# Shift and scale columns of a transformer's modulation made with the weights in the array, from four weight buffers

## What is computed

```python
for l in range(DEPTH):                       # DEPTH = 2
    m_lat = jnp.split(cond_lat @ w_mod[l] + b_mod[l], 6, axis=-1)
    m_ctx = jnp.split(cond_ctx @ w_mod[l] + b_mod[l], 6, axis=-1)
    y_lat, y_ctx = _token_mixing(            # w_in, attention, delta net, HGRN, w_out
        _modulate(x_lat, m_lat[0], m_lat[1]), _modulate(x_ctx, m_ctx[0], m_ctx[1]), ...)
    x_lat = x_lat + m_lat[2] * y_lat
    x_lat = x_lat + m_lat[5] * _expert_choice_ffn(_modulate(x_lat, m_lat[3], m_lat[4]), ...)
    ...                                      # the same for x_ctx, in the first layer

def _modulate(x, shift, scale):
    return _rms(x) * (1 + scale) + shift
```

## Time and profile before

| | us |
|---|---|
| median of 3 runs | 3901.55 |
| lowest, highest | 3899.71, 3906.54 |
| the profiled execution, its own time | 3915.78 |
| its span, first to last instruction | 3914.0 |
| PE busy in the span | 3239.1 |
| PE weight loads busy | 2335.5 |
| DVE busy | 2296.5 |
| ACT busy | 1742.8 |

### The profile page before, as it was taken

How to read it: one execution, slowest core, us unless ns; L and a number is a source line. 1 busy time by engine, 2 the same in 40 slices (tenths; PEclk the granted TensorE clock), 3 DMA queues, 4 the chain that set the end, 5 groups by cost and what they waited for, 6 DMA issues and landing times.

```text
span 3914.0 us, 59293 instructions
## 1 busy us (share of the span) xinstructions
PE 3239.1 (83%) x24115; PEld 2335.5 (60%) x24115; DVE 2296.5 (59%) x2989; ACT 1742.8 (45%) x2289; POOL 359.9 (9%) x100
## 2 busy tenths in 40 slices
PE   6899977766859998989988999787658588888887
PEld 1465767655436666666642566677554466666666
DVE  0140564677247777777741043555782678788887
ACT  1111531223136777767740114422231477777776
POOL 0000000000011112111100000000000122222122
PEclk9999977856979999999999999888558788888888
DMA  7310000001167988889865110000002589898996
GB/s 248 111 49 32 1 1 3 3 2 45 41 238 286 354 333 322 327 322 353 323 244 204 44 54 1 1 3 3 2 33 113 224 327 343 330 347 341 346 347 252
DMA packets 180704, 680.24 MB, mean 174 GB/s; under 512 B 15435, under 2 KB 25759, under 8 KB 180383
## 3 DMA queue, kind: packets, MB, share of 16 engines
q1 hardware_dynamic: 166088, 637.81, 42.9%
q0 software_dynamic: 6144, 20.98, 2.3%
q10 hardware_dynamic: 8283, 18.67, 1.2%
HBM read 656.44 MB, written 20.97 MB: 173 GB/s over the span
## 4 chain that ended last, share of the span: by engine, by line
PE 65%; DVE 14%; DMA 8%; ACT 6%; issue 6%; ACTq 1%; SPq 0%; POOL 0%; DVEq 0%; PEldq 0%
PE ps L1835 14%; PE ps L718 13%; PE ps L1865 11%; PE ps L1290 5%; DMA gu<-in_moe_w_gate 4%; PE ps L1635 4%; PE ps L657 3%; PE ps L1873 2%; PE ps L973 2%; ACT hi L1947 2%; DMA arena<-in_w_mod 2%; DMA gu<-in_moe_w_up 2%; DVE gu_lo L2096 2%; PE ps L951 1%; PE ps L964 1%
## 5 line engine op out<-in xcount | busy, mean ns | idle before, releaser
L2096 DVE TENSOR_TENSOR gu_lo<-gu,hi 128x2816 fp32r<-128x2816 f32 x256 | 781.4, 3086 | 327.7 <-ACT hi L1947 289.5
L1947 ACT ACTIVATE hi<-gu 128x2816 fp32r<-128x2816 f32 x256 | 643.0, 2551 | 192.4 <-DMA gu<-in_moe_w_up 147.7
L1835 PE MATMUL ps<-hi,xsplit 128*96 128x512 f32 (+3 forms) x2304 | 602.3, 410 | 73.7 <-ACT hi L1947 53.0
L1835 PEld LDWEIGHTS ps<-hi,xsplit 128*96 128x96 f32 (+1 forms) x2304 | 425.3, 190 | 198.6 <-ACT hi L1947 63.7
L718 PE MATMUL ps<-arena 128*128 128x512 f32 (+2 forms) x1536 | 503.4, 488 | 7.3 <-PE ps L718 4.5
L2096 DVE TENSOR_TENSOR down_lo<-down,hi 128x1024 fp32r<-128x1024 f32 (+1 forms) x256 | 404.0, 1619 | 64.0 <-ACT hi L1947 64.0
L1835 PE MATMUL ps<-gu_lo,xsplit 128*96 128x512 f32 (+3 forms) x1536 | 400.9, 399 | 40.8 <-DVE gu_lo L2096 40.8
L1947 ACT ACTIVATE hi<-down 128x1024 fp32r<-128x1024 f32 (+1 forms) x256 | 347.5, 1375 | 177.8 <-PE ps L1865 127.5
L718 PEld LDWEIGHTS ps<-arena 128*128 128x128 f32 x1536 | 289.7, 190 | 212.5 <-issue 187.2
L1835 PEld LDWEIGHTS ps<-gu_lo,xsplit 128*96 128x96 f32 (+1 forms) x1536 | 280.2, 188 | 134.4 <-DVE gu_lo L2096 70.9
L2176 POOL DMA_INDIRECT arena<-xn_rows,row_of x32 | 53.2, 1662 | 2158.0 <-DVE row_of L2087 2153.4
(11 more groups left out here) (290 smaller groups left out, 4453.3 us busy)
## 6 DMA issues: line engine op xcount, KB each, us to landing
gu<-in_moe_w_gate SPq DMA_DIRECT2D x256, 704.0 KB, 13.6
gu<-in_moe_w_up SPq DMA_DIRECT2D x256, 704.0 KB, 5.2
down<-in_moe_w_down SPq DMA_DIRECT2D x64, 2048.0 KB, 13.2
arena<-in_w_mod SPq DMA_DIRECT2D x24, 2048.0 KB, 8.1
down<-in_moe_w_down SPq DMA_DIRECT2D x32, 1536.0 KB, 17.3
arena<-in_w_in SPq DMA_DIRECT2D x6, 2048.0 KB, 8.0
arena<-in_w_out SPq DMA_DIRECT2D x4, 2048.0 KB, 10.2
arena<-in_w_in SPq DMA_DIRECT2D x4, 1536.0 KB, 6.8
```

Of the source, the lines that this page charges most:

```text
L1835: ins = nc.tensor.matmul(ps[0:lhs.shape[1], 3 * m + b, 0:n], lhsT=lhs, rhs=w[:, c0 + 512 * b:c0 + 512 * b + n], start=(row == 0 and stage ...
L1947: nc.scalar.activation(hi_part(p, is_last), whole(p), ACT.Copy).then_inc(hi_a.sem, 1)
L2096: nc.vector.tensor_tensor(lo_part(p), whole(p), hi_part(p, is_last).bitcast(F32), ALU.subtract) \
```

## The change

The 12 chunks now have four buffers of their own, `mst`, with a semaphore each, and SP waits for `modmm`, the count of finished chunks, without TensorE's own wait between. The loads of `w_in` wait for the chunks that lie in the same memory (9 and 10). The four gate chunks are multiplied as before. The eight shift and scale chunks are multiplied the other way round: each 128 x 128 block of the weights is the stationary operand and the two conditions are the moving one, so that a chunk is 4 blocks times 8 slices, 32 matmuls with 2 columns each, and the result is already columns over 128 partitions. Their bias is added from `rowsT`, into which `b_mod` is now transposed at the start together with the other small rows, in one DVE step per part; the 32 transposes and `modT` go. DVE does two gate rows, the columns, and the last two gate rows, in this order. On ACT the loads are cut in two: constants, conditions and the `b_mod` rows first, then Silu and the copy, and only then x, ctx and the small parameters. Three constants that nothing reads are dropped.

```diff
-        for g, (src, n) in enumerate(loads(layer)):
...
+                if layer:
+                    sp.wait_ge(used.sem, used.n(layer - 1, USES * NE))
+                for g in range(N_MOD):
+                    if g >= MRING:
+                        sp.wait_ge(modmm.sem, modmm.n(layer, g - MRING + 1))
                     if g == 2:
                         for r in range(2):
                             sp.dma_start(modrow[r:r + 1, :], t["b_mod"][layer:layer + 1, :]).then_inc(bmod.sem, 16)
+                    sp.dma_start(mst[g % MRING], t["w_mod"][layer][:, g * 512:(g + 1) * 512]
+                                 .rearrange("(f p) n -> p f n", p=P)).then_inc(mload[g % MRING].sem, 16)
...
-            for n, (dst, src) in enumerate(ins):
-                act.dma_start(dst, src).then_inc((s_first if n < N_FIRST else s_in).sem, 16)
+            for dst, src in ins[:N_FIRST]:
+                act.dma_start(dst, src).then_inc(s_first.sem, 16)
             act.wait_ge(s_rowsT.sem, 1)
-            nc.scalar.activation(rowsT[:, :], ps[:, 7, 0:84], ACT.Copy).then_inc(s_cond.sem, 1)
             nc.scalar.activation(condT[:, :], ps[:, 7, 68:84], ACT.Silu).then_inc(s_cond.sem, 1)
+            nc.scalar.activation(rowsT[:, :], ps[:, 7, 0:84 + DEPTH * 48], ACT.Copy).then_inc(s_cond.sem, 1)
+            for dst, src in ins[N_FIRST:]:
+                act.dma_start(dst, src).then_inc(s_in.sem, 16)
...
-                for f in range(KT):
-                    ins = nc.tensor.matmul(ps[0:2, g % 2, :], lhsT=cT[:, f, :], rhs=w[:, f, :],
-                                           start=(f == 0), stop=(f == KT - 1))
+                if g in GATE_CHUNKS:
...
+                        ins = nc.tensor.matmul(ps[0:2, n % 2, :], lhsT=cT[:, f, :], rhs=w[:, f, :],
+                                               start=(f == 0), stop=(f == KT - 1))
+                else:
+                    for b in range(4):
+                        at = 2 * (MOD_COLUMNS.index(g // 2) * KT + 4 * (g % 2) + b)
+                        for f in range(KT):
+                            ins = nc.tensor.matmul(ps[:, 2, at:at + 2], lhsT=w[:, f, b * P:(b + 1) * P], rhs=cT[:, f, :],
+                                                   start=(f == 0), stop=(f == KT - 1))
                 ins.then_inc(modmm.sem, 1)
-
-                pe.wait_ge(modmm.sem, modmm.n(layer, g + 1))
-                pe.sem_inc(wfree.sem, 1)
-            pe.wait_ge(modadd.sem, modadd.n(layer, N_MOD))
-            for m, part in enumerate((0, 1, 3, 4)):
-                for f in range(KT):
-                    c0 = part * D + f * P
-                    at = 2 * (m * KT + f)
-                    ins = nc.tensor.transpose(ps[:, 6, at:at + 2], modrow[0:2, c0:c0 + P], ident[0:2, 0:2])
-            ins.then_inc(modT.sem, 1)
+            pe.wait_ge(modcol.sem, modcol.n(layer, 1))
+            pe.wait_ge(modadd.sem, modadd.n(layer, len(GATE_CHUNKS)))
```

More of the change, by code:

```diff
@@ L42 @@
 N_MOD = 6 * D // 512
-N_IN = 7 + 7 * DEPTH
-N_FIRST = 5
-LOADS = N_MOD + len(GROUPS) + 2
+N_IN = 8 + 7 * DEPTH
+N_FIRST = 6
+LOADS = len(GROUPS) + 2
 WRING = 2
+MRING = 4
+MOD_COLUMNS = (0, 1, 3, 4)
+GATE_CHUNKS = [g for g in range(N_MOD) if g // 2 not in MOD_COLUMNS]
+LAST_COLUMN_CHUNK = max(g for g in range(N_MOD) if g // 2 in MOD_COLUMNS)
 X_AT = 43616
@@ L71, in _layout @@
                     ("incl0", 128), ("incl1", 128), ("chunkind", 256), ("causal0", 64), ("causal1", 64),
-                    ("iota", 64), ("before", 128), ("after", 128), ("ident64", 64), ("cc", 256), ("ss", 256)):
+                    ("ident64", 64), ("cc", 256), ("ss", 256)):
         CONST[name] = (at, n)
@@ L113, in constants @@
     put("causal1", s64 >= t64)
-    put("iota", t64)
-    put("before", c < p)
-    put("after", c > p)
     put("ident64", s64 == t64)
@@ L152, in trunk_program @@
         const = sb("const", [P, N_CONST])
-        rowsT = sb("rowsT", [P, 84])
+        rowsT = sb("rowsT", [P, 84 + DEPTH * 48])
         condT = sb("condT", [P, 2 * KT])
@@ L212, in trunk_program @@
         rows = view(42000, P)[0:84, :]
+        rows_b = view(42128, P)[0:DEPTH * 48, :]
         ident = cst("ident")
@@ L226, in trunk_program @@
         modrow = view(18944, 6144)
+        mst = [view(at, KT, 512) for at in (6144, 10240, 14336, 25088)]
         xn = ycat
@@ L319, in trunk_program @@
         bmod = sem("bmod", 32)
+        mload = [sem(f"mload{i}", 16 * N_MOD // MRING) for i in range(MRING)]
         modmm = sem("modmm", N_MOD)
-        modadd = sem("modadd", N_MOD)
-        modT = sem("modT", 1)
+        modadd = sem("modadd", len(GATE_CHUNKS))
         modcol = sem("modcol", 1)
@@ L472, in loads @@
         def loads(layer):
-            w_mod, w_in, w_out = t["w_mod"], t["w_in"], t["w_out"]
-            for g in range(N_MOD):
-                yield w_mod[layer][:, g * 512:(g + 1) * 512], 512
+            w_in, w_out = t["w_in"], t["w_out"]
             for c0, n, _ in GROUPS:
@@ L514, in sync_program @@
                             sp.dma_start(modrow[r:r + 1, :], t["b_mod"][layer:layer + 1, :]).then_inc(bmod.sem, 16)
+                    sp.dma_start(mst[g % MRING], t["w_mod"][layer][:, g * 512:(g + 1) * 512]
+                                 .rearrange("(f p) n -> p f n", p=P)).then_inc(mload[g % MRING].sem, 16)
+                for g, (src, n) in enumerate(loads(layer)):
+                    k = layer * LOADS + g
+                    if g < WRING:
+                        sp.wait_ge(modmm.sem, modmm.n(layer, N_MOD - MRING + g + 1))
+                    if k >= WRING:
+                        sp.wait_ge(wfree.sem, k - WRING + 1)
+                    if g == len(GROUPS):
+                        sp.wait_ge(houtv.sem, houtv.n(layer, 2 * len(out_tiles(layer))))
                     sp.dma_start(wst[k % WRING][:, :, 0:n], src.rearrange("(f p) n -> p f n", p=P)) \
@@ L636, in tensor_program @@
             pe.wait_ge(s_first.sem, 16 * N_FIRST)
-            nc.tensor.transpose(ps[:, 7, 0:84], rows[:, :], ident[0:84, 0:84]).then_inc(s_rowsT.sem, 1)
-            pe.wait_ge(s_cond.sem, 2)
+            nc.tensor.transpose(ps[:, 7, 0:84], rows[:, :], ident[0:84, 0:84])
+            nc.tensor.transpose(ps[:, 7, 84:84 + DEPTH * 48], rows_b, ident[0:DEPTH * 48, 0:DEPTH * 48]) \
+                .then_inc(s_rowsT.sem, 1)
+            pe.wait_ge(s_cond.sem, 1)
             for layer in range(DEPTH):
@@ L707, in pe_proj @@
                 if g != last_g:
-                    w, last_g = staged(pe, layer, N_MOD + g), g
+                    w, last_g = staged(pe, layer, g), g
                 if u >= 6:
@@ L760, in dve_mod, with gate_row @@
             dve.wait_ge(bmod.sem, bmod.n(layer, 32))
-            for g in range(N_MOD):
+            def gate_row(n):
+                g = GATE_CHUNKS[n]
                 dve.wait_ge(modmm.sem, modmm.n(layer, g + 1))
[L763 to L773, removed]
+                nc.vector.tensor_tensor(gates[:, n // 2, (n % 2) * 512:(n % 2) * 512 + 512], ps[0:2, n % 2, :],
+                                        modrow[0:2, g * 512:(g + 1) * 512], ALU.add).then_inc(modadd.sem, 1)
+            gate_row(0)
+            gate_row(1)
+            dve.wait_ge(modmm.sem, modmm.n(layer, LAST_COLUMN_CHUNK + 1))
+            for m, part in enumerate(MOD_COLUMNS):
+                src = ps[:, 2, 16 * m:16 * m + 16].rearrange("p (f v) -> p f v", v=2)
+                at = 84 + 48 * layer + KT * part
+                bias = rowsT[:, at:at + KT].unsqueeze(2).broadcast_to([P, KT, 2])
+                ins = nc.vector.scalar_tensor_tensor(modC[:, m, :, :], src, float(m % 2), bias, ALU.add, ALU.add)
             ins.then_inc(modcol.sem, 1)
+            gate_row(2)
+            gate_row(3)
         def dve_norm(dve, layer, which):
@@ L1628, in pe_out @@
             for g in range(2):
-                w = staged(pe, layer, N_MOD + len(GROUPS) + g)
+                w = staged(pe, layer, len(GROUPS) + g)
                 for n, i in enumerate(outs):
```

10 lines of the change are left out of this document (7 added, 3 removed).

## The result

The changed kernel takes 3954.85 us (median of 4 runs, 3943.18 to 3957.87), the kernel before 3900.63 (4 runs, 3893.87 to 3906.54): a ratio of 1.0133 with a 95% interval of 1.0112 to 1.0154, so 44 to 60 us more. The profiled execution took 3957.87 us, its span is 3956.1. The forecast was 3961, with a range of 3930 to 3992.

The account below looks back on a forecast made before the run. TensorE was taken to bound the modulation stretches, with load waits the rest. First layer +21.6 and second +37.7 gave +59.3 us: 3975.1 for the profiled execution, 3960.9 (3961) as a median, range 3930 to 3992.

Parts of the forecast that it names:

- The form of a record: Column chunks: one weight load with its 2-column matmul costs 0.2133 us at half clock, so 13.65 us a chunk.
- The bounds of 0.163 and 0.24: Column chunks: lower and upper limits in us for a half-clock record, from 30 transposes and from eight loads.
- Rivals 3 and 4: Column chunks: half-clock records cost 0.163 us, total 3910, chance 0.06; or 0.24 us, total 3988, chance 0.06.
- rival 3: Column chunks: half-clock records cost as little as cold transposes, 0.163 us, total 3910; chance 0.06.
- The other bounds: Whole kernel: records at 0.196, start at 19.3 or a longer rest of full clock give 3936 to 3970 us.
- The clock: Column chunks: TensorE's granted clock is 0.50, since weight loads do not hold it up; gate chunks bring it to 1.00.
- rival 1: Column chunks: loads hold the clock up, records cost 0.1125 us, total -38.4 us, 3863; chance 0.05.
- Rival 2: Column chunks: clock falls, but a load takes about 0.107 us at either clock, total -38 us, 3863; chance 0.05.
- Start: First layer: TensorE begins the chunks at 12.0 us in place of 31.24, bounds 11 and 19.3.
- Chunks 0 to 3: First four column chunks of each layer: all at half clock, 4 x 13.65 = 54.6 us.
- Gates: Gate chunks 4 and 5: begin at half clock and bring it up, 9.0 + 7.0 = 16.0 us.
- Chunks 6 to 9: Last four column chunks: three us at full clock, then half, 54.6 - 3 = 51.6 us.

Follow-up runs that it names:

- e2: Changed kernel with 64 moving columns in place of 2 on each weight block of the column chunks; 3903.72 us, ratio 1.0011.
- e7: Changed kernel with 128 moving columns in place of 2 on each weight block of the column chunks; 3866.88 us, ratio 0.9915.
- e11: Changed kernel with 64 moving columns and two column chunks, then gate chunks 4 and 5, ahead of the other column chunks; 3876.41 us, ratio 0.9929.
- e1: Changed kernel with shift and scale multiplied as rows again, keeping four buffers and early conditions; 3875.39 us, ratio 0.9931.
- e3: As e1, rows with early conditions, but two weight buffers in place of four; 3889.58 us, ratio 0.9978.
- e9: As e8, with row chunks cut into two halves that can run side by side in the array; 3845.97 us, ratio 0.9865.
- e8: As e1, with ACT making the Exp of the lower bounds before it issues the late loads; 3866.96 us, ratio 0.9915.
- e10: As e2, with 64 moving columns, but gate chunks 4 and 5 put first in the order; 3968.98 us, ratio 1.0171.

## Why the prediction was right

**The form of a record.** Taken: 0.2133 us at half clock, with the rows with 4 columns at 533 us as the nearest in form. No run shows 0.2133 itself: those rows have 0.196 for eight records, and 0.2145 stands in the earlier trace rows with 64 columns. Measured: 54.74 and 54.78 for 256, 0.214. The bounds of 0.163 and 0.24 were both far off; PE's rows, 0.196 and 0.2145, were the better witness than single spans of PEld, which overlap each other (the next begins at 537.51, the eight end at 537.63). Rivals 3 and 4 fall by it.

The lower bound was a misreading, and so was the ground of rival 3: the earlier trace rows are not at half clock throughout. The windows over these transposes, in the kernel before:

```profile
135.30:138.50 3.20, 3.18 (x15) 3.18 (x16) 0.24 (x1) 1.23 (x2) 0.00 (x0) 0.50 0.01 3
138.70:142.00 3.30, 3.30 (x30) 2.94 (x29) 2.76 (x5) 2.47 (x4) 0.00 (x0) 1.00 0.00 0
```

The 30 loads from 135.32 to 140.21 lie across the change: a record takes 0.21 us (15 in 3.18) at 0.50 and 0.11 (30 in 3.30) at 1.00, and the 0.163 is a mean over both. So nothing in the rows spoke for a record of 0.163, and nothing shows transposes to be "another kind of pass": their records are as long as those of the column chunks, 0.214 and 0.112. The other bounds add up to 3937 and 3968, not quite the 3936 and 3970 written; nothing hangs on that.

**The clock.** Taken from the earlier trace rows: loads do not hold it. The windows above show 0.50 over both column stretches of the second layer, and rival 1 falls. That the small number of moving columns is the cause is shown by e2: chunks 6 to 9 begin at full clock behind gate chunks in both kernels, and with 2 columns the clock falls (0.50 over 2103 to 2153 us), with 64 it stays (1.00 over 2079 to 2107 in e2). e7 and e11 add that the same loads run at either level with nothing altered but that number and the order. Rival 2 falls by the windows above, a record of 0.214 us at 0.50, and by e2, with 0.112 at 1.00 for the same loads, where it had about 0.107 at both clocks.

**The terms.** Start 12.0, measured 12.30. Chunks 0 to 3: 54.6, measured 54.7. Gates: 16.0, measured 16.3 (the 9.0 in it rests on the second layer of before, where the chunk of 8.96 us begins at 0.50, 2025.7 to 2028; the first layer's 9.48 us stand under a printed 1.00). Chunks 6 to 9: 51.6, measured 52.6; the rest of full clock, 1.00 from 83.3 to 85.5 us, gave back two us and not three. Gates again: 16.0, measured 16.0. Norm at 150.9, measured 152.6. Second layer, request to norm: 148.6 (2015.97 to 2164.6), measured 149.9.

**The sum.** The stretches give 23.3 + 39.0 = 62.3 us where 59.3 were forecast. The medians differ by 54, with an interval that ends at 60, and the two profiled executions by 42. Where the last 20 us are can be told: between the first norm and the second request the profile before has 1886.7 us and the profile after 1867.4. In the experiments' profiles that stretch is 1885.1 for e1 and 1865.0 for e3, both with rows, and 1863.4 for e11 with columns, so it varies between profiles by about the amount that is missing, and not with the form of the matmuls. 17.6 of the 19.2 us lie in the first layer's experts, whose work is the same in both kernels; PE's waits there, before and after, hold 10 of them:

```profile
PE ps L1893 <- DVE arena L2146: 48.4, 16, 4.4
```

```profile
PE ps L1914 <- DVE arena L2167: 38.3, 16, 4.1
```

Why they differ is open. What remains between 62 by the stretches and 54 by the medians is not settled: in nine of the ten kernels measured against it the median's difference lies 2 to 12 us below what the two stretches give, in e9 5 above, and one profile of the kernel before is too few to say whether its other parts are slower or that execution was. It changes no sign. But that the forecast lies within 6 us of the medians is in part luck: its terms were 3 us too small together, and 8 that no term held went the other way.

**What was missed, hidden by what was right.** The text gave the small parameters "tens of us" and no price. In fact ACT's issuing of them lasts until 36.6, ahead of the Exp on which DVE waits with its first bias rows. Under the slow column chunks, which need nothing from DVE until chunk 10, it cost nothing; with rows TensorE stood idle behind it for 9.8 us (e1), and 5.6 of them came back when the Exp was moved (e8). A step that is moved has to be followed to the engine that waits behind it also when the forecast says that it is covered, since the cover is then to be named. The same holds for the third chunk's weights: with four loads and x in flight they land at 34 to 35 us, which half-clock chunks never notice and every quick version does (e7, e8, and in e10 the gap that cost 50).

## What to carry to other kernels

Before turning a matmul round so that the large operand is stationary, count its weight loads at half clock: here a stream of loads with 2 moving columns did not keep TensorE at full clock (0.50 over 50 us of it), and the records slowed down with it (0.214 us for 0.112), so that the doubled cost fell on the very thing that the new form is made of. Moving columns that nobody needs can be cheap insurance: at half clock 64 cost no more than 2 (0.214 us a record), and at full clock 128 no more than 64 (0.112). But look at where the clock is when they begin: 64 held a full clock here and left it at half after a gap, and only 128 also brought it up. When a slow stage hides waits, price them anyway; whoever quickens that stage meets them at once.

## What the runs showed of the hardware that was not expected

- 64 moving columns on each 128 x 128 block held a full clock over 43 us (e11) but left it at half for 109 us where it began there (e10); 128 columns brought it up from half within some 5 us (e7, twice). With 2 columns it fell from 1.00 to 0.50 within some 2.3 us (changed kernel, chunks from 83.3 and from 2100.7 us).
- A record of a 128 x 128 weight load in 32-bit floats with its matmul took 0.112 us at full clock (e2, e7, e11) and 0.214 at half (changed kernel, e2, e10), the first with 64 or 128 moving columns, the second with 2 or 64.
- Transposes of 128 x 128 blocks alone brought the clock from half to full after some 3 us (kernel before, 0.50 over 135.3 to 138.5 us, 1.00 from 138.7).
- Matmuls with two stationary columns each, on different halves of the array, ran side by side: eight with 512 moving columns took 3.60 us (e9), where they take 7.03 in a row (e3).
- DMA into the buffers of the row chunks ran at 386 GB/s over 36 us (e9), the window that follows, with TensorE busy for 25 of them.

```profile
54.00:90.00 36.00, 24.95 (x114) 4.52 (x112) 14.30 (x21) 7.63 (x13) 0.00 (x0) 1.00 1.05 386
```
